# Four instead of three seven-product pairs per up-projection chunk, with one weight sum made by adding DMAs

## The reference, cut to what matters

```
def swiglu(x, wg, wu, wd):
    return (jax.nn.silu(x @ wg) * (x @ wu)) @ wd

f = swiglu(rmsnorm(h, ffn1_pre_g[l]), ffn1_wg[l], ffn1_wu[l], ffn1_wd[l])
h = h + FFN_RES_WEIGHT * rmsnorm(f, ffn1_post_g[l])
```

## Time and profile before

| | us |
|---|---|
| median of 3 runs | 2091.24 (2089.2 to 2092.17) |
| the profiled execution, its own time | 2091.08 |
| its span, first to last instruction | 2089.3 |
| DVE busy | 1680.8 |
| ACT busy | 1112.4 |
| POOL busy | 28.8 |

### The profile page before, as it was taken

How to read it: one execution, slowest core, us unless ns; L and a number is a source line. 1 busy time by engine, 2 the same in 40 slices (tenths; PEclk the granted TensorE clock), 3 DMA queues, 4 the chain that set the end, 5 groups by cost and what they waited for, 6 DMA issues and landing times.

```text
span 2089.3 us, 25938 instructions
## 1 busy us (share of the span) xinstructions
PE 2070.9 (99%) x9322; PEld 1712.3 (82%) x9322; DVE 1680.8 (80%) x2049; ACT 1112.4 (53%) x1252; POOL 28.8 (1%) x54
## 2 busy tenths in 40 slices
PE   9999999999999999999999999999999999999998
PEld 7788888888878788888788888888888888888886
DVE  6788889888988657998687555578899888889885
ACT  6455555557545454444465444465555555565553
POOL 0000000000000000100000000000000000000000
PEclk9999999999999999999999999999999999999999
DMA  8656655666656566776555566556666665656564
GB/s 285 199 190 212 202 190 192 201 202 194 198 191 222 165 184 194 203 207 185 173 168 182 184 190 209 192 177 196 201 199 202 201 197 185 203 199 210 185 211 160
DMA packets 211995, 409.51 MB, mean 196 GB/s; under 512 B 15113, under 2 KB 15377, under 8 KB 211520
## 3 DMA queue, kind: packets, MB, share of 16 engines
q1 hardware_dynamic: 209904, 401.26, 59.9%
q0 software_dynamic: 1856, 7.01, 1.5%
q10 hardware_dynamic: 144, 0.04, 0.0%
HBM read 406.14 MB, written 2.11 MB: 195 GB/s over the span
## 4 chain that ended last, share of the span: by engine, by line
PE 97%; DVE 1%; issue 1%; DMA 1%; ACT 0%; POOL 0%; SPq 0%; DVEq 0%; ACTq 0%; POOLq 0%
PE banks L1537 95%; PE banks L1587 2%; DVE wlo L956 0%; DMA raw<-in_ffn_wg_dram 0%; DMA raw<-in_ffn_wd_dram 0%; DVE res L1009 0%; POOL stat L430 0%; ACT act_hi L532 0%; DVE act_lo L1022 0%; DVE comb L1168 0%; ACT junk L596 0%; DVE comb L980 0%; ACT whi L517 0%; SPq L349 0%; PE banks L1827 0%
## 5 line engine op out<-in xcount | busy, mean ns | idle before, releaser
L517 ACT ACTIVATE whi<-raw 128x1024 fp32r<-128x1024 f32 x755 | 780.2, 1053 | 742.4 <-PE banks L1537 388.1
L956 DVE TENSOR_TENSOR wlo<-raw,whi 128x1024 fp32r<-128x1024 f32 x756 | 900.1, 1217 | 266.3 <-ACT whi L517 263.2
L1537 PE MATMUL banks<-whi,act_hi 128*128 128x512 f32 x1688 | 542.3, 395 | 5.1 <-issue 3.8
L1537 PE MATMUL banks<-whi,act_lo 128*128 128x512 f32 x1688 | 532.5, 390 | 0.0
L1537 PE MATMUL banks<-wlo,act_hi 128*128 128x512 f32 x1688 | 522.8, 390 | 0.4 <-DVE wlo L956 0.4
L1537 PEld LDWEIGHTS banks<-whi,act_hi 128*128 128x128 f32 x1688 | 313.8, 188 | 72.2 <-issue 9.4
L1537 PEld LDWEIGHTS banks<-wlo,act_hi 128*128 128x128 f32 x1688 | 317.0, 188 | 67.4 <-DVE wlo L956 1.4
L1537 PEld LDWEIGHTS banks<-whi,act_lo 128*128 128x128 f32 x1688 | 317.2, 188 | 66.8
L1537 PE MATMUL banks<-whi,h_hi 128*128 128x512 f32 x560 | 179.2, 390 | 1.2 <-DVE comb L1168 1.2
L1537 PE MATMUL banks<-whi,h_lo 128*128 128x512 f32 x560 | 178.9, 389 | 0.0
L1537 PE MATMUL banks<-wlo,h_hi 128*128 128x512 f32 x560 | 175.1, 389 | 0.0
(11 more groups left out here) (239 smaller groups left out, 2019.7 us busy)
## 6 DMA issues: line engine op xcount, KB each, us to landing
raw<-in_ffn_wg_dram SPq DMA_DIRECT2D x176, 512.0 KB, 3.7
raw<-in_ffn_wu_dram SPq DMA_DIRECT2D x176, 512.0 KB, 4.5
raw<-in_ffn_wd_dram SPq DMA_DIRECT2D x176, 512.0 KB, 4.6
raw<-in_w_in_dram SPq DMA_DIRECT2D x160, 512.0 KB, 3.6
raw<-in_w_out_dram SPq DMA_DIRECT2D x32, 512.0 KB, 3.6
raw<-in_w_pw_dram SPq DMA_DIRECT2D x16, 512.0 KB, 3.7
raw<-in_w_o_dram SPq DMA_DIRECT2D x16, 512.0 KB, 4.2
x_t<-in_x_tiles_dram SPq DMA_DIRECT2D x8, 256.0 KB, 6.9
```

What stands on the lines that cost most here:

```text
L517: nc.scalar.activation(whi[:, j % RING, 0:kts * width], raw[:, j % RING, 0:kts * width], ACT.Copy).then_inc(hi_ready, 1)
L956: nc.vector.tensor_tensor(wlo[:, j % RING, 0:n], raw[:, j % RING, 0:n], whi[:, j % RING, 0:n], ALU.subtract).then_inc(lo_ready, 1)
L1537: return nc.tensor.matmul(o, a, b, **kw)
```

## The change

- `SEVEN` becomes `(1, 2, 4, 5)`: four of eight pairs of every up-stage chunk use seven products. The activations' sums follow, with one scratch buffer `afull` in place of three, and `asum` in the place of `asum_lo`.
- P of these pairs is no longer made by DVE. SP loads b12 (256 KB) into `wsum[i]`, one of four buffers, beside the slab loads (`P_WITH` says after which slab); POOL waits for it and issues a DMA that adds b11 (256 KB) onto it. DVE waits for the adding DMA (`p_full`), then makes R, the in-place sum and Z. The down stage keeps its four sums on DVE.
- In the up stage `hidden` moves to q = 2, and in chunk 1 `hidden_of_first` goes ahead of the sums of q = 1.
- `FRONT` opens with two plain pairs instead of one.
- At the end of a feed-forward layer `gain_tile` goes ahead of the request for the factor. Between the first feed-forward layer and the mixing layer PE transposes the residual after three of the four last slabs instead of two, and ACT and DVE do slab 2 of the next sublayer before the second tile's norm.

```
-SEVEN = (1, 3, 5)
+SEVEN = (1, 2, 4, 5)
+P_WITH = {0: (0,), 1: (1,), 3: (2,), 5: (3,)}
-FRONT = [q for two in zip(PLAIN, DOWN_SEVEN) for q in two]
+FRONT = PLAIN[:1] + [q for two in zip(PLAIN[1:], DOWN_SEVEN) for q in two]
...
@@ SP, ffn
                     for j in range(UP_SLABS):
                         load(j, rows(w_up[f][j % 2])[:, j // 2 * SK:j // 2 * SK + SK, bass.ts(c, CW)],
                              base + UP_SLABS * c + j - RING + 1)
+                        for i in P_WITH.get(j, ()):
+                            if not (f == 0 and isinstance(c, int) and c == 1):
+                                sp.wait_ge(wsumlo_ready, seven_before(f, c, i) - len(SEVEN) + 1)
+                            sp.dma_start(wsum[i][:, P_SUM, :], rows(w_up[f][1])[:, SK * SEVEN[i], bass.ts(c, CW)]).then_inc(p_loaded[i], 16)
...
@@ POOL
+            def summed(f):
+                def one(c, group):
+                    for i, q in enumerate(SEVEN):
+                        pool.wait_ge(p_loaded[i], 16 * (SUMMED * f + c))
+                        pool.dma_start(wsum[i][:, P_SUM, :], rows(w_up[f][0])[:, SK * q, bass.ts(c, CW)],
+                                       accum_op=ALU.add).then_inc(p_full[i], 16)
+                return one
             pool.wait_ge(mm_done, UP_SLABS)
             load_gpost(f1_post)
+            summed_chunks(pool.Fori, summed(0))
             root(2, rpost[0])
...
@@ ACT, start_phase
                     if p == 1:
+                        hi_at(2)
                         act_hi_half(p, 2, 0, 1)
                         chunk_squares(*LAST[p - 1], 1)
...
@@ DVE, finish
                     if sub != 1:
                         last_add(sub, 0)
+                        link(gain_tile(sub, buf, BLK - 1, 0))
...
@@ DVE, start_phase
                         last_add(0, 1)
+                        lo_at(2)
+                        finish(0, 1)
                         split(2, 0, 1)
-                        finish(0, 1)
...
@@ DVE, weight_sums
-                    nc.vector.tensor_tensor(wsum[:, P_SUM, :], b11, b12, ALU.add).then_inc(wsum_ready, 1)
-                    dve.wait_ge(wsum_ready, 4 * seven + 1)
-                    nc.vector.tensor_tensor(wsum[:, R_SUM, :], wsum[:, P_SUM, :], b22, ALU.add).then_inc(wsum_ready, 1)
+                    if added is None:
+                        dve.wait_ge(wsumlo_ready, seven)
+                        link(nc.vector.tensor_tensor(low[:, P_SUM, :], b11, b12, ALU.add))
+                    else:
+                        dve.wait_ge(*added)
+                    nc.vector.tensor_tensor(low[:, R_SUM, :], low[:, P_SUM, :], b22, ALU.add).then_inc(wsum_ready, 1)
...
@@ DVE, summed
+                        if q == SEVEN[0] and first:
+                            hidden_of_first()
                         if q in SEVEN:
                             weight_sums(seven, base // RING + UP_SLABS // RING * c + 2 * q // RING + 1, 2 * q % RING,
-                                        first and f == 0 and q == SEVEN[0])
+                                        wsum[i], (p_full[i], 16 * (SUMMED * f + c)))
...
-                        if q == SEVEN[0]:
-                            if first:
-                                hidden_of_first()
-                            else:
-                                hidden(c - 1)
+                        if q == 2 and not first:
+                            hidden(c - 1)
...
@@ PE, last_slabs
-                    if j == 1 and p < 3:
+                    if j == (2 if p == 1 else 1) and p < 3:
                         act_half(p, 0, 0, 1)
                         act_half(p, 1, 0, 1)
...
@@ PE, down stage, second half
-                    if i == 1:
+                    if i == 2:
                         pe.wait_ge(combined, combined_count(f, SUMMED + 1, 5))
```

More of the change, by code:

```diff
@@ L569, in start_phase @@
                         act_hi_half(p, 2, 0, 1)
-                    hi_at(2)
+                        hi_at(2)
                     hi_at(3)
@@ L681, in quad @@
                     if q in DOWN_SEVEN:
-                        act.wait_ge(wsum_ready, 4 * seven + 3)
+                        act.wait_ge(wsum_ready, 3 * seven + 2)
                     hi_at(n + 1)
                     if q in DOWN_SEVEN:
-                        act.wait_ge(wsum_ready, 4 * seven + 4)
+                        act.wait_ge(wsum_ready, 3 * seven + 3)
                         act.wait_ge(wsum_used, seven)
-                        nc.scalar.activation(wsum_hi[:], wsum[:], ACT.Copy).then_inc(wsumhi_ready, 1)
+                        nc.scalar.activation(wsum_hi[:], wsum0[:], ACT.Copy).then_inc(wsumhi_ready, 1)
                 def outer_copies(half):
@@ L996, in finish @@
                 if t == 0:
-                    link(gain_tile(sub, buf, BLK - 1, t))
+                    if sub == 1:
+                        link(gain_tile(sub, buf, BLK - 1, t))
                     dve.wait_ge(acc_free[1 - buf], LEFT[sub][1 - buf])
@@ L1131, in hidden, with weight_sums, weight_sums_lo @@
                     ins.then_inc(hidden_ready, 1)
[L1133 to L1138, removed]
+                def weight_sums(seven, loads, slot, low, added):
+                    for n in slot, slot + 1:
+                        dve.wait_ge(raw_full[n], 16 * loads)
                     b11, b21 = raw[:, slot, 0:CW], raw[:, slot, CW:2 * CW]
                     b12, b22 = raw[:, slot + 1, 0:CW], raw[:, slot + 1, CW:2 * CW]
-                    nc.vector.tensor_tensor(wsum[:, P_SUM, :], b11, b12, ALU.add).then_inc(wsum_ready, 1)
-                    dve.wait_ge(wsum_ready, 4 * seven + 1)
-                    nc.vector.tensor_tensor(wsum[:, R_SUM, :], wsum[:, P_SUM, :], b22, ALU.add).then_inc(wsum_ready, 1)
+                    if added is None:
+                        dve.wait_ge(wsumlo_ready, seven)
+                        link(nc.vector.tensor_tensor(low[:, P_SUM, :], b11, b12, ALU.add))
+                    else:
+                        dve.wait_ge(*added)
+                    nc.vector.tensor_tensor(low[:, R_SUM, :], low[:, P_SUM, :], b22, ALU.add).then_inc(wsum_ready, 1)
                     nc.vector.tensor_tensor(b12, b12, b22, ALU.add).then_inc(wsum_ready, 1)
-                    dve.wait_ge(wsum_ready, 4 * seven + 2)
-                    nc.vector.tensor_tensor(wsum[:, Z_SUM, :], wsum[:, R_SUM, :], b21, ALU.add).then_inc(wsum_ready, 1)
-                def weight_sums_lo(seven, low=wsum_lo):
+                    dve.wait_ge(wsum_ready, 3 * seven + 1)
+                    nc.vector.tensor_tensor(low[:, Z_SUM, :], low[:, R_SUM, :], b21, ALU.add).then_inc(wsum_ready, 1)
+                def weight_sums_lo(seven, full, low=wsum_lo):
                     dve.wait_ge(wsumhi_ready, seven + 1)
-                    nc.vector.tensor_tensor(low[:], wsum[:], wsum_hi[:], ALU.subtract).then_inc(wsumlo_ready, 1)
+                    nc.vector.tensor_tensor(low[:], full[:], wsum_hi[:], ALU.subtract).then_inc(wsumlo_ready, 1)
                 def combine(c, group):
@@ L1174, in summed @@
                         seven = seven_before(f, c, SEVEN.index(q)) if q in SEVEN else None
+                        if q == SEVEN[0] and first:
+                            hidden_of_first()
                         if q in SEVEN:
+                            i = SEVEN.index(q)
+                            if not (first and f == 0):
+                                dve.wait_ge(wsumlo_ready, seven - len(SEVEN) + 1)
                             weight_sums(seven, base // RING + UP_SLABS // RING * c + 2 * q // RING + 1, 2 * q % RING,
-                                        first and f == 0 and q == SEVEN[0])
+                                        wsum[i], (p_full[i], 16 * (SUMMED * f + c)))
                         if q == SEVEN[0] and not first:
```

55 lines of the change are left out of this document (32 added, 23 removed).

## The result

The kernel after takes **2112.5 us** (median of 4 runs, 2109.0 to 2113.0) against 2091.7 (2089.2 to 2092.9) for the kernel before: a ratio of 1.0096, 95% interval 1.008 to 1.0112. The prediction was 2083.5, and its range ended at 2103.

The account below looks back on a forecast made before the run. PE, busy 99% of the span, was taken as the bound. From 2091.08 us: matmuls -13.6, late slab 3 +7.2, chunk 1 +1.5, second layer's chunk 1 -0.4, half -1.2, layer end -1.1 gave 2083.5 us, range 2074 to 2103.

Parts of the forecast that it names:

- DVE pair by pair: Up stage, q = 1 to 3: DVE finishes slab 6's `lo` 0.55 us before PE needs it; later slips make PE wait.
- term (a): Up stage, chunks 2 to 10: adding DMAs delay slab 3's load to 5.3 us; PE waits 0.4 per chunk, +7.2 us.
- w = landing - 4.9: PE's wait per up-stage chunk, from slab 3's load time issue to landing; 0.4 us at the assumed landing of 5.3.
- T0: The moment in each up-stage chunk when DVE starts the sums of q = 1; PE opens q = 1 6.42 us later.
- The slack: Slab 3's load is issued 4.32 us before DVE's sums of q = 1, plus 0.55 margin: landings to 4.9 cost nothing.
- crowded loads: Rival, up stage: slab 3 lands at 5.7 us or more; at 6.4 PE waits 1.5 per chunk, 2103 us; chance 0.2.
- A late add: Rival, up stage: adding DMA takes over about 5.7 us and delays DVE's sums; 2107 us at 8.0; chance 0.12.
- The rule of two source reads: Skill's rule: an adding DMA moves at half a copy's rate, worth 1.3 us of transfer; sum 2094.3 us instead of 2083.5.
- rule on the lock of GpSimd: Skill's rule: certain DVE instructions lock GpSimd out of writing DMA descriptors, which would make the adding DMA late; no size given.
- The matmuls: Up stage: 3 matmuls fewer per chunk, 0.68 us, in ten chunks of each of two layers: -13.6 us.
- Chunk 1: First layer: first add lands behind the gains at about 60 us, PE waits 5.3 and the clock falls: +1.5 us.
- Half and layer ends with the second layer's chunk 1: Down-stage half -1.2 us, end of first layer -1.1, pause in the second layer's chunk 1 -0.4.

Follow-up runs that it names:

- e16: Kernel after with the last two of the four `combine` steps moved behind the low parts of slabs 14 and 15: 2103.7 us.
- e4: Kernel before with only the changes of order (`hidden_of_first`, `FRONT`, `gain_tile`, sublayer end), three sevens and P on DVE: 2081.8 us.
- e1: Kernel after with P loads and adding DMAs in chunk 1 of each layer alone (output partly wrong, for timing only): 2087.0 us.
- e8: Kernel after with P loads and adds in chunk 1 of each layer alone, and `hidden` moved behind q = 3 (timing only): 2080.5 us.
- e7: Kernel after with POOL issuing chunk 1's adds of the first layer ahead of the load of gains: 2102.7 us.
- e18: Kernel after with earlier P loads, chunk 1's adds before gains, `hidden` behind q = 3, P of q = 4 and 5 on DVE, and `combine` split: 2101.7 us.
- e17: Kernel after with earlier P loads, chunk 1's adds ahead of gains, `hidden` behind q = 3, and `combine` split: 2083.2 us.
- e3: Kernel after with each adding DMA replaced by a plain copy of the same 256 KB on the same queue (timing only): 2098.9 us.

## Why the prediction was wrong

**The step that failed: DVE pair by pair, with term (a).** The forecast's w = landing - 4.9 had the right form, and the predicted end of the `lo` of slab 6, T0 + 16.3, is where it is (1582.19 - 1565.90). Two sizes were off.
- *The landing*: 5.3 taken, 6.5 measured on average. 18 x 1.2 = 21.6 us. I priced one ordinary 256 KB transfer in the way; each add counts almost double and, with one or two in flight with slab 3, the load took up to 8.7.
- *The slack*: 4.9 taken, 4.53 measured, 18 x 0.37 = 6.7 us. I wrote that T0 "starts afresh from PE in every chunk". After the change it does not: DVE's wait of 2.08 us for ACT is still there, but behind it DVE waits 1.1 to 4.3 us more for slab 3's load, whose issue comes from DVE's own low part of slab 15. The wait of 2.4 us before `combine` that decoupled DVE from this ring was part of the 42.4 us that I averaged over as idle time. I had also read the step from one chunk, 1466.26, in which the load was not late; in 13 of the 18 it already was, by up to 0.71 us.

Together 28.3 us, of the 29.2 by which the term was off: it was +7.2 in the sum and measured +36.4. The whole forecast missed by 29.0.

**The rival "crowded loads" is what happened**, at a mean landing of 6.5, near the 6.4 for which it gave 2103; with w = landing - 4.53 it would have given 2091.1 - 14.8 + 18 x 2.0 = 2112. It had 0.2. **A late add** did not set T0 in chunks 2 to 10 of the kernel after, but it was the next in line, as e16 shows: P load and add took 4.0 + 0.6 + 7.7 us there, where the prediction allowed 4.6 + 0.7 + 5.7.

**The rule of two source reads** (Trainium skill, Collectives: The Full Stack, "The bandwidth ceiling: the fold count and why AG ≠ RS ≠ AR"): the trace agrees, 14.2% against 7.2% of the engines for the same bytes, and 13.6 us. By it the sum would have been 2094.3, for a landing of 5.9; the landing of 6.5 and the smaller slack made up most of the rest, 18 x 0.6 + 6.7 = 17.5 us.
The Trainium skill's rule on the lock of GpSimd (SBUF — State Buffer, "SBUF: two separate sides") changed nothing that a run here shows: 76 of POOL's 80 instructions for an add took 0.85 to 0.89 us, with DVE at work around them.

**What held.** The matmuls: 60 fewer. Chunk 1: the add behind the gains landed at 60.4 (predicted 60), PE waited 5.9 us (5.3) and the clock fell; the first transposes come at 95.4 against 93.7, +1.7 with the chunk's three matmuls less (-0.7) in it, so +2.4 where +1.5 was predicted. Half and layer ends with the second layer's chunk 1: 3.0 us gained between the two up stages, 0.7 of it that chunk's three matmuls, so 2.3 where 2.7 was predicted.

**The account**, in us, from the runs: order of work -9.6 (e4); matmuls -13.6 (the prediction's price, not run by itself); the 0.53 us per chunk that e1 keeps, 18 x 0.53 = +9.5 (e8 takes 6.5 of it back); chunk 1's add behind the gains +9.8 (e7); P loads +1.7; copies +10.2; adding +13.6. Sum +21.6, measured +20.8. Each part carries some 2 us of noise, so the agreement is closer than it can be trusted. The parts are not independent: where one ring is cut, the next takes over, as e16 to e18 show.

**Left open.** Which wait holds e17 above 41.7 us in half of its chunks was not taken apart. Nor was its chunk 1: in the profiled execution its transposes come at 94.9 us where e4's come at 87.0, behind two waits of PE of 1.57 and 2.16 us and a granted clock of 0.86 from 70 to 80. A fifth slot for slabs, which would loosen the first ring, was not tried.

## What to carry to other kernels

An engine that is busy 90% of a period can be without slack if a load stands in its loop: add its work from one start to the release of the buffer, add the transfer that it waits for, and compare that sum, not the busy time, with the period. Look for all such rings before shortening one: here a cut of 1.45 us gave 0.5, since the second ring was that close. And count a DMA that adds as two transfers (1.9 here), in the place where it is in flight beside a load that is just in time.

## What the hardware showed that was not expected

- An adding DMA of 256 KB from DRAM onto SBUF landed in 5.8 us at the median, a copy of the same bytes on the same queue in 4.3. The adds of the up stage were 5184 packets, the copies 2830.
- Shortly behind an add's issue the DMA engines are busy but move little. Two stretches of 1 us of the kernel after, behind the add that POOL issues at 182.82 (the last two columns are the DMA share and GB/s; a whole chunk before had 0.62 and 198):
```profile
183.20:184.20 1.00, 1.00 (x10) 1.00 (x9) 0.95 (x1) 0.00 (x0) 0.49 (x1) 1.00 0.59 166
184.20:185.20 1.00, 1.00 (x6) 0.79 (x6) 0.00 (x0) 0.89 (x1) 0.00 (x0) 1.00 0.71 63
```
  Slab 3's load, issued at 184.17, took 8.7 us there.
- The issuing instruction on POOL takes 0.85 to 0.89 us for an add (76 of 80; the three issued in a row behind the gains, from 52.45, took 0.94, 1.27 and 1.63), 0.54 to 0.59 for e3's copies of the same size, and 0.72 for the 1 MB load of gains.
